# Layout of the gated expert weights in a PEER retrieval stage: high and low parts apart instead of interleaved, with the half tile's pair joined by a small copy

## The reference, cut to what matters

```python
e = ...            # (T, 8 heads, 16) numbers of the chosen experts, of 128 * 128
g = softmax(sc)    # their gates
def one_chunk(args):
    xc, ec, gc = args
    u = expert_u[ec]
    a = gelu(einsum('cd,chkd->chk', xc, u))
    return einsum('chk,chkd->cd', gc * a, expert_v[ec])
```

## Time and profile before

| | |
|---|---|
| median of three runs | 1551.1 us |
| profiled execution, first to last instruction | 1549.6 us |
| TensorE busy | 1466.4 us (95%) |
| VectorE busy | 1326.8 us (86%) |
| ScalarE busy | 673.2 us (43%) |
| GpSimd busy | 787.1 us (51%) |
| TensorE's mean granted clock | 0.983 of full speed |

### The profile page before, as it was taken

How to read it: one execution, slowest core, us unless ns; L and a number is a source line. 1 busy time by engine, 2 the same in 40 slices (tenths; PEclk the granted TensorE clock), 3 DMA queues, 4 the chain that set the end, 5 groups by cost and what they waited for, 6 DMA issues and landing times.

```text
span 1549.6 us, 25331 instructions
## 1 busy us (share of the span) xinstructions
PE 1466.4 (95%) x7847; PEld 1261.3 (81%) x7847; DVE 1326.8 (86%) x2654; ACT 673.2 (43%) x1255; POOL 787.1 (51%) x733
## 2 busy tenths in 40 slices
PE   4999999999989778889999999999999999999996
PEld 3777767868577577779999999999999999999995
DVE  5878645346999989799999999999999999999998
ACT  5232456322157567534444434444444444444443
POOL 1010000000059857677767667767667667667662
PEclk8999999999999989999999999999999999999998
DMA  9895211440021256899999999999999999999994
GB/s 344 317 388 193 81 55 55 149 181 1 1 110 55 75 227 258 339 402 402 401 397 401 398 369 403 390 375 402 391 365 402 396 377 402 381 379 402 383 384 157
DMA packets 164991, 448.84 MB, mean 290 GB/s; under 512 B 14683, under 2 KB 50675, under 8 KB 164284
## 3 DMA queue, kind: packets, MB, share of 16 engines
q1 hardware_dynamic: 108732, 243.33, 42.4%
q0 software_dynamic: 56192, 204.66, 33.7%
HBM read 423.72 MB, written 22.32 MB: 288 GB/s over the span
## 4 chain that ended last, share of the span: by engine, by line
PE 78%; DVE 13%; DMA 3%; issue 2%; ACT 2%; POOL 1%; SPq 0%; ACTq 0%; DVEq 0%; POOLq 0%
PE bank L942 15%; PE bank L1205 9%; PE bank L1204 9%; PE bank L1203 9%; PE bank L1227 7%; PE bank L1225 7%; PE bank L1226 7%; PE bank L1217 4%; PE bank L1218 4%; PE bank L1125 2%; PE bank L1038 2%; DMA w_scratch<-staged 1%; PE bank L885 1%; DVE top_i L1937 1%; DVE scores L1938 1%
## 5 line engine op out<-in xcount | busy, mean ns | idle before, releaser
L778 POOL DMA_INDIRECT v_rows<-v_exp,small x192 | 258.0, 1344 | 91.2 <-POOL small L774 51.0
L778 POOL DMA_INDIRECT u_rows<-u_exp,small x192 | 255.9, 1333 | 92.8 <-POOL small L774 52.0
L1203 PE MATMUL bank<-h_hi,u_hi 128*128 128x320 f32 x944 | 291.1, 308 | 0.7 <-ACT staged L1500 0.7
L1204 PE MATMUL bank<-h_lo,u_hi 128*128 128x320 f32 x944 | 291.7, 309 | 0.0
L1205 PE MATMUL bank<-h_hi,u_lo 128*128 128x320 f32 x944 | 291.7, 309 | 0.0
L1227 PE MATMUL bank<-v_hi,g_both 128*128 128x512 f32 x512 | 204.2, 399 | 0.0
L1603 ACT ACTIVATE v_hi<-v_raw 128x1024 fp32r<-128x1024 f32 x128 | 135.5, 1058 | 157.6 <-PE bank L1227 116.4
L1225 PE MATMUL bank<-v_hi,g_both 128*128 128x512 f32 x512 | 203.2, 397 | 0.0
L1226 PE MATMUL bank<-v_lo,g_both 128*128 128x512 f32 x512 | 203.2, 397 | 0.0
L1204 PEld LDWEIGHTS bank<-h_lo,u_hi 128*128 128x128 f32 x944 | 177.1, 188 | 6.2
L1203 PEld LDWEIGHTS bank<-h_hi,u_hi 128*128 128x128 f32 x944 | 177.2, 188 | 5.7 <-ACT staged L1500 0.9
(11 more groups left out here) (255 smaller groups left out, 2923.6 us busy)
## 6 DMA issues: line engine op xcount, KB each, us to landing
v_raw<-v_exp SPq DMA_DIRECT2D x128, 512.0 KB
u_raw<-u_by_key SPq DMA_DIRECT2D x120, 512.0 KB
ada_blk<-ada_w SPq DMA_DIRECT2D x22, 1024.0 KB, 10.9
ring<-w_in SPq DMA_DIRECT2D x18, 1024.0 KB, 10.1
w_row<-w_scratch SPq DMA_DIRECT2D x128, 128.0 KB
w_scratch<-staged SPq DMA_DIRECT2D x2, 4096.0 KB, 17.0
xr<-x SPq DMA_DIRECT2D x8, 512.0 KB, 6.3
ring<-w_branch SPq DMA_DIRECT2D x4, 1024.0 KB, 5.1
```

Source lines behind the costliest of these rows:

```text
L778: pool.indirect_dma_start(out=rows[s], out_offset=None, in_=table, in_offset=bass.IndirectOffsetOnAxis(ap=ix[:, s:s + 1], axis=0))\
L1203: pe.matmul(o, u_hi[:, r, k], h2_hi[:, k], start=(k == 0), stop=False)
L1204: pe.matmul(o, u_hi[:, r, k], h2_lo[:, k], start=False, stop=False)
```

## The change

The buffer becomes `g_all[128, 2 buffers, 704]`: for each of the two buffers the 320 high parts, then a gap of 64 words, then the 320 low parts. The weights of a full tile are then 128 neighbouring words. The 64 high parts of the half tile stand at the end of the high run, and the gap behind them is filled by a new copy of the 64 low parts of the half tile (`g_pair`), so that high and low lie side by side there too. ScalarE makes this copy at the end of its block step, after it has waited for VectorE's low part. TensorE does the half tile's four products last in a block instead of first, behind a new wait for this copy (`g_paired`).

Some things follow from it: the two halves of the half tile's result now stand one above the other and not interleaved, so one `fold` matrix serves both tails (one VectorE instruction less); and since the half tile's products are the last of the last block, ScalarE waits for all three counts of `y_full` before the copies `y_parts`.

```diff
-        g_both = at("g_both", 177, [P, 2, DS, 2], F32R)
+        g_all = at("g_all", 176.5, [P, 2, 2 * DS + EX], F32R)
-        fold = at("fold", 32, [P, 2, EX])
+        fold = at("fold", 32, [P, EX])
+        def g_hi(r):
+            return g_all[:, r, 0:DS]
+        def g_pair(r):
+            return g_all[:, r, DS - EX:DS + EX]
+        def g_lo(r):
+            return g_all[:, r, DS + EX:2 * DS + EX]
...
@@ TensorE, second
-                both = g_both[:, r, DS - EX:DS].rearrange("p t a -> p (t a)")
-                for f in range(2):
-                    o, half = banks[2 * (DT - 1) + f][:, :], slice(f * HALF, (f + 1) * HALF)
-                    pe.matmul(o, both, v_hi[:, r, half], start=is_first, stop=False)
-                    last = pe.matmul(o, both, v_lo[:, r, half], start=False, stop=is_last)
-                if is_last:
-                    last.then_inc(y_full, 1)
                 for t in range(DT - 1):
-                    hi, lo = (g_both[:, r, t * P:(t + 1) * P, a] for a in range(2))
+                    hi, lo = (g[:, t * P:(t + 1) * P] for g in (g_hi(r), g_lo(r)))
...
-                if not is_last:
-                    last.then_inc(v_done, 1)
+                pe.wait_ge(g_paired, j + 1)
+                for f in range(2):
+                    o, half = banks[2 * (DT - 1) + f][:, :], slice(f * HALF, (f + 1) * HALF)
+                    pe.matmul(o, g_pair(r), v_hi[:, r, half], start=is_first, stop=False)
+                    last = pe.matmul(o, g_pair(r), v_lo[:, r, half], start=False, stop=is_last)
+                last.then_inc(y_full if is_last else v_done, 1)
...
@@ ScalarE, block_step and the end
-                act.activation(g_both[:, r, :, 0], gated[:, r], ACT.Copy).then_inc(g_hi_done, 1)
+                act.activation(g_hi(r), gated[:, r], ACT.Copy).then_inc(g_hi_done, 1)
                 if not isinstance(b, int) or b + 1 < NK:
                     half_gates(n, c + 1)
                     v_high(n, c + 1)
+                act.wait_ge(g_lo_done, b + 1)
+                act.activation(g_pair(r)[:, EX:P], g_lo(r)[:, DS - EX:DS].bitcast(F32), ACT.Copy).then_inc(g_paired, 1)
...
-            act.wait_ge(y_full, 1)
+            act.wait_ge(y_full, DT)
             for f in range(2):
                 act.activation(y_parts[:, f * HALF:(f + 1) * HALF], banks[2 * (DT - 1) + f][:, :], ACT.Copy)\
                     .then_inc(parts_copied, 1)
             for t in range(DT):
-                if t < DT - 1:
-                    act.wait_ge(y_full, t + 2)
...
@@ VectorE, block_step and once in the first blocks
-                dve.tensor_tensor(g_both[:, r, :, 1], gated[:, r], g_both[:, r, :, 0].bitcast(F32), ALU.subtract)\
+                dve.tensor_tensor(g_lo(r), gated[:, r], g_hi(r).bitcast(F32), ALU.subtract)\
-            two = ident.rearrange("p (t a) -> p t a", a=2)
-            dve.tensor_tensor(fold[:, 0], two[:, :, 0], two[:, :, 1], ALU.add)
-            dve.tensor_tensor(fold[:, 1], ident[:, 0:EX], ident[:, EX:P], ALU.add).then_inc(fold_ready, 1)
+            dve.tensor_tensor(fold, ident[:, 0:EX], ident[:, EX:P], ALU.add).then_inc(fold_ready, 1)
```

More of the change, by code:

```diff
@@ L494, in build @@
         h2x_in, ex_ready, ex_in, ex_placed = (sem(n) for n in ("h2x_in", "ex_ready", "ex_in", "ex_placed"))
-        fold_ready, parts_copied, folded = sem("fold_ready"), sem("parts_copied"), sem("folded")
+        fold_ready, parts_copied, folded, g_paired = (
+            sem(n) for n in ("fold_ready", "parts_copied", "folded", "g_paired"))
         idx_u_set, idx_v_set, u_rows_in, v_rows_in, u_rows_used, v_rows_used = (
@@ L1253, in _ @@
                 half = slice(f * HALF, (f + 1) * HALF)
-                pe.matmul(banks[6 + f][EX:P, :], fold[:, 1], acc_x[:, half], start=True, stop=True)
+                pe.matmul(banks[6 + f][EX:P, :], fold, acc_x[:, half], start=True, stop=True)
                 pe.wait_ge(parts_copied, f + 1)
-                pe.matmul(banks[6 + f][0:EX, :], fold[:, 0], y_parts[:, half], start=True, stop=True).then_inc(folded, 1)
+                pe.matmul(banks[6 + f][0:EX, :], fold, y_parts[:, half], start=True, stop=True).then_inc(folded, 1)
         @block.scalar
```

## The result

The changed kernel takes 1541.2 us in the median of five runs (1539.9 to 1542.6), against 1550.7 us for the kernel before on the same chip: a ratio of 0.993, 95% interval 0.9919 to 0.9940. That is 9.5 us faster. The forecast was 1547.7 us, the range 1537 to 1552 with 0.38 for faster, so the sign of the likeliest number, the range and the place of the gain held, and its size was nearly three times what I had taken. The time also lies under the border of 1546.4 us, so the outcome that I had thought likeliest, the same within 0.3% (0.55), did not come.

What follows compares the result with a forecast made beforehand. TensorE was taken to bound the kernel. Terms -3.4 (stepped weights), 0, -0.1 and +0.1 sum to -3.4 us against the 1549.6 us span, giving 1546.2, and 1547.7 us as median; range 1537 to 1552 us.

Steps and rivals of the forecast that it cites:

- What bounds it: In the expert blocks' stage TensorE, busy 60.00 of 60 us, sets the pace; one block's `second` takes 3.74 us for 16 products.
- The stepped weights: Full tiles' 12 products in `second` each lose 2.7 ns; 23 to 32 ns a block, about 123 blocks, -3.4 us.
- the far bound: All 16 products of `second` reach the mixing half's 226.7 ns: 113 ns a block, 13.9 us over 123 blocks.
- the slow last interval: Last product of `second` to next `first`: 241 ns against 233 to 235; 9 ns of the gain might not come.
- Rival A: Full tiles' 2.7 ns belong to their way through two banks, so nothing comes back: 1551.3 us, chance 0.15.
- Rival B: All the stage's 512-column products fall to 226.7 ns: 1537.2 us, chance 0.19.
- The order and the new wait: In `second`, moving the half tile's products and adding a semaphore wait costs TensorE nothing: 0, at most 0.9 us.
- The copy: ScalarE's 128 copies of 238 ns fit its idle time: 0, with 1.3 us to spare where no `first` stands between blocks.
- Rival C: TensorE waits for the late copy at eight places without a `first` between: 1555.7 us, chance 0.09.
- One `fold` fewer: VectorE, which TensorE waits for near 664 us, has one instruction less: -0.1 us.
- the end: `y_parts` waits for TensorE's last product and moves about 0.6 us, partly hidden behind L2221: 0 to +0.6, taken as +0.1.
- DMA: In the expert blocks' stage its share is 1.01 already, and it would have to keep up with 1.6% shorter blocks.

## Why the prediction was right or wrong

**What bounds it.** Right. TensorE paces the stage, and 88 ns less in its block came through for each block of the steady stage.

**The stepped weights, -3.4 us with bounds 0 and -13.9.** This step failed by its size. I priced the step by the half tile's four products, 231.7 ns, as "the value of the half tile's products, as they have the same moving operand and stand in the same stage". They also stood right behind the 320-column products, and there neighbouring weights lose 21 ns over the first four products and 25 over the first five. The step's true price is 6.7 ns a product and not 2.7: 233.4 against 226.7 ns with nothing else running. The pace of the earlier trace rows, which I had as the far bound, was the right one to price by; it is the steady pace of 512 columns with neighbouring weights in a fast place. The prediction named this as a sign that it is wrong: "if the half tile's products, with weights as before, change their own pace". They did, from 231.7 to 226.7 ns, so the gain falls in the stated range for a reason that my sum did not have. The size also hangs on something that the prediction doesn't name and met by luck, the place where the words begin: with the buffer one word on, the same change brings 2.3 us.

The measured balance is this. Before: 16 products at 226.7 ns are 3.627 us; the kernel had 3.740, 113 ns more, from stepped weights, the place behind `first` and the slow last interval. The order alone takes 32 ns off (3.740 to 3.708): the half tile's four products give 17.5 of it and the twelve stepped ones 14, half of which is the slow last interval. The stepped products, when they stand behind `first`, show 232 to 233 ns like everywhere else, so the two prices don't add, and the half tile is all but free of both. The layout takes off 12 * 6.7 = 80 ns, and the 25 ns of the place behind `first` appear again: 55 net, and 56 measured (3.708 to 3.652). 32 + 56 = 88 ns.

**Rival A** (nothing to be had back): wrong here. By the Trainium skill (SBUF — State Buffer, the cachelines note in the section "Door 1: The DMA port swizzle") two fp32 words in each 16 bytes are free. The trace of TensorE alone differs with 512 moving columns, 6.7 ns a product, and agrees with 320, where it shows nothing. The step of four words, one in each 16 bytes, costs no more than that of three (234.8 and 235.5 ns). **Rival B** (1537.2 us) was the mechanism, with 113 ns a block; it missed the 25 ns behind `first`, and 2 us of new waits at the start. I had given it 0.19 and held against it that the neighbouring products beside took 231.7 ns; what that row showed was their place. I also wrote that the stepped weights "could slow the four products around them as well", and that part is not so: with nothing stepped near them, in the kernel of products alone, they take the same 0.93 us together behind the 320-column ones. The last interval of `second`, of which I thought that 9 ns might stay, is 241 ns only where stepped products are last; with the half tile last it is 226.7.

**The order and the new wait, 0.** The wait costs nothing, right. The order was worth 32 ns in a common block, 2.6 us alone, and I had 0: I compared products before and after by their number and banks and not by what stands in front of them.

**The copy, 0 with a cover of 1.3 us.** Right, by the run with the order and the copy. At the tight place the copy ends at 1032.18 us and TensorE comes to the half tile at 1033.43, 1.25 us later. **Rival C** did not come; its cover is real, since without it the same copy costs 12 us.

**One `fold` fewer, -0.1, and the end, +0.1.** The end came out at +0.1. The wait near 664 us was to be 0.1 us shorter and ended 0.3 us later; VectorE's low part there hangs on gathered rows that came later (its own wait for them is 1.3 us, 0.8 before). VectorE is 0.44 us later in front of the `fold` instructions (664.82 against 664.38 us) and 0.30 behind them (666.09 against 665.79), so the one fewer did give its 0.14 us.

**DMA.** I named it as an argument against rival B only. It took a part: at the start of the stage the blocks of U come later and TensorE waits in two blocks. That this comes from the faster pace isn't shown, and one run speaks against it: with the order and the copy, at the old pace, ScalarE waits 20.4 us for U, TensorE stands twice (0.3 and 0.5 us) and the run of blocks there takes 1.25 us more than a later one. With the order alone ScalarE waits 15.2 us for U, and TensorE has no such wait.

## What to carry to other kernels

To price a change in how TensorE reads its weights, compare starts of products with the same neighbours: the first five products behind a row of shorter or misplaced ones are slower by themselves. Keep the stationary operand's 128 words neighbouring, and try where they begin: here the fast beginnings lay 256 bytes apart, and since the address itself was not at a multiple of 256 bytes, another kernel should measure its own. With 512 moving columns a step of two words, or a start 64 bytes off, costs 3% of the products' pace, and with 320 columns neither costs anything. When a layout change brings a copy, the place of its consumer decides whether the copy is free: the same copy cost 0 behind twelve other products and 12 us in front of them.

## What the runs showed of the hardware

- An fp32r product of 512 columns in a steady row, its weights 128 neighbouring words in a fast place, takes 226.7 ns at the full clock (2.4 GHz level), 320 columns 146.7 ns and 384 columns 173.3 ns: 13.3 ns more than one column a cycle in each case.
- 512 columns with weights stepped by 2, 3, 4, 7 and 8 words: 233.4, 235.5, 234.8, 239.1 and 246.2 ns.
- Neighbouring weights that begin off a multiple of 64 words, counted from the tile's beginning: 229 to 233 ns, also at 4, 8, 16 and 32 words.
- The first five of such products at a fast place take 25 ns more together behind 320-column products; behind misplaced 512-column ones the first four intervals are the same 236, 229, 232 and 231 ns.
- The profile's duration of the weight load is 188 ns in the fast and in the misplaced case alike, and 193 to 196 ns with a step of two; with steps of 4 and more it passes 300 ns while the starts of the products move by 8 to 20 ns.
- With nothing else on the chip a block's 16 products take the same 3.74 and 3.71 us as beside DMA at a share of 1.0 and VectorE busy for 57 of 60 us.
